# Four layers in one kernel: the high part of gate and query weights meets both parts of h in one product of 512 columns

## The reference

```python
h = _layernorm(x) * (1.0 + scale[:, None, :]) + shift[:, None, :]
p = h @ w_in[l]
u_f, z_f, cq, ckv, k_r, z_a = jnp.split(p, split_pts, axis=-1)
y_f = _fourier_mix(u_f, w_fmix[l]) * jax.nn.silu(z_f)
...
y_a = _mla_attention(q_nope, q_rope, k_nope, k_rope, v) * jax.nn.silu(z_a)
y = jnp.concatenate([y_f, y_a], axis=-1) @ w_out[l]

h = rms_norm(x, norm_g) @ w_in          # even: pooling, top-k attention
p_in, p_gate, dq, dk, dv, d_gate, iq, ik, iw = split_cols(h, EVEN_SPLITS)
h = rms_norm(x, norm_g) @ w_in          # odd: windowed attention with sinks
q, k, v, gate = split_cols(h, ODD_SPLITS)
```

## Time and profile before

| | |
|---|---|
| Median of three runs | 1638.18 us (1636.6 to 1639.8) |
| The profiled execution | 1637.07 us |
| Its span, first to last instruction | 1635.3 us |
| Busy: PE, PE weight loads, DVE, ACT | 1508.8, 1329.6, 1086.4, 706.7 us |
| Mean granted TensorE clock | 0.965 of 2.4 GHz |
| Read from HBM | 341.16 MB, 210 GB/s |
| Chain that ended last, by engine | PE 78%, DVE 8%, DMA 5%, ACT 4% |

### The profile page before, as it was taken

The page is one execution under the profiler, slowest core; times in us unless marked ns, Lnnn a source line. Parts: engine busy times, 40 slices in busy tenths (PEclk is TensorE's granted clock), DMA queues, the critical chain, the costliest instruction groups (busy, mean ns, idle before and its releaser), DMA issues.

```text
span 1635.3 us, 25215 instructions
## 1 busy us (share of the span) xinstructions
PE 1508.8 (92%) x9919; PEld 1329.6 (81%) x9919; DVE 1086.4 (66%) x1854; ACT 706.7 (43%) x1195; POOL 30.7 (2%) x56
## 2 busy tenths in 40 slices
PE   4888999989949999999968999999998999999998
PEld 0667788988839888998858998789987998879986
DVE  3426668889987757666676466884655667886553
ACT  1324234335326444444325344544544545655442
POOL 3000000000000000000000000010000000000000
PEclk8898999999979999999988999999999999999999
DMA  9996887998945766676546546427665553434662
GB/s 351 380 380 230 256 288 252 368 330 331 346 155 170 255 168 200 226 244 207 193 141 197 174 142 177 133 73 262 184 193 153 167 155 104 115 106 140 183 218 90
DMA packets 182437, 345.00 MB, mean 211 GB/s; under 512 B 28876, under 2 KB 43440, under 8 KB 181552
## 3 DMA queue, kind: packets, MB, share of 16 engines
q1 hardware_dynamic: 177744, 326.88, 61.7%
q0 software_dynamic: 4576, 16.52, 2.9%
HBM read 341.16 MB, written 2.20 MB: 210 GB/s over the span
## 4 chain that ended last, share of the span: by engine, by line
PE 78%; DVE 8%; DMA 5%; ACT 4%; issue 3%; SPq 2%; POOLq 0%; POOL 0%; DVEq 0%; ACTq 0%
PE PM L1359 65%; PE PB L1359 8%; DMA stg<-in_w_in 3%; SPq L1284 2%; ACT AR L1709 2%; DMA AR<-in_w_in 1%; ACT whi L1709 1%; DVE X L1934 1%; PE PB L1561 1%; PE PB L1533 1%; DVE AC L1934 1%; PE PB L1636 1%; DMA AR<-in_w_ada 1%; DVE wlo L2010 1%; DVE AR L1934 1%
## 5 line engine op out<-in xcount | busy, mean ns | idle before, releaser
L2010 DVE TENSOR_TENSOR wlo<-stg,whi 128x1024 fp32r<-128x1024 f32 (+2 forms) x421 | 500.1, 1197 | 350.3 <-ACT whi L1709 349.0
L1709 ACT ACTIVATE whi<-stg 128x1024 fp32r<-128x1024 f32 (+2 forms) x421 | 434.2, 1037 | 467.4 <-PE PM L1359 352.2
L1359 PE MATMUL PM<-Hh,whi 128*128 128x256 f32 x1824 | 528.0, 292 | 9.1 <-DVE wlo L2010 6.6
L1359 PE MATMUL PM<-Hh,wlo 128*128 128x256 f32 x1780 | 501.5, 285 | 0.0
L1359 PE MATMUL PM<-Hl,whi 128*128 128x256 f32 x1824 | 498.1, 285 | 0.0
L1359 PEld LDWEIGHTS PM<-Hh,whi 128*128 128x128 f32 x1824 | 353.2, 194 | 28.8 <-issue 12.4
L1359 PEld LDWEIGHTS PM<-Hh,wlo 128*128 128x128 f32 x1780 | 344.1, 193 | 0.0
L1359 PEld LDWEIGHTS PM<-Hl,whi 128*128 128x128 f32 x1824 | 343.1, 193 | 0.6
L1359 PE MATMUL PM<-whi,Hh 128*128 128x512 f32 (+1 forms) x576 | 224.3, 391 | 0.0
L1359 PE MATMUL PM<-wlo,Hh 128*128 128x512 f32 (+1 forms) x576 | 220.9, 385 | 0.0
L1359 PE MATMUL PM<-whi,Hl 128*128 128x512 f32 (+1 forms) x576 | 219.1, 385 | 0.0
(11 more groups left out here) (268 smaller groups left out, 1461.3 us busy)
## 6 DMA issues: line engine op xcount, KB each, us to landing
stg<-in_w_ada SPq DMA_DIRECT2D x162, 512.0 KB, 6.5
stg<-in_w_in SPq DMA_DIRECT2D x107, 512.0 KB, 5.4
stg<-in_even_w_in SPq DMA_DIRECT2D x80, 512.0 KB, 3.6
stg<-in_odd_w_in SPq DMA_DIRECT2D x72, 512.0 KB, 3.7
stg<-in_w_out SPq DMA_DIRECT2D x64, 512.0 KB, 5.0
stg<-in_even_w_out SPq DMA_DIRECT2D x32, 512.0 KB, 3.9
stg<-in_odd_w_out SPq DMA_DIRECT2D x32, 512.0 KB, 4.2
AR<-in_w_ada SPq DMA_DIRECT2D x30, 512.0 KB, 11.5
```

The lines of the kernel that those rows point to most:

```text
L1359: return e.matmul(out, l, r, start=start, stop=stop, skip_group_check=True)
L1709: return e.activation(out, x, f, **k)
L2010: e.tensor_tensor(wlo[s["slot"]][:, :, 0:n], stg[s["slot"]][:, :, 0:n], whi[s["hi"]][:, :, 0:n].bitcast(F32), ALU.subtract).then_inc(SEM[" ...
```

## The change

H becomes one tensor `H2` with the two parts of a k block side by side, so that 512 columns hold Hh and Hl of it. In a **wide** group the whi weights of a block stream over all 512 of them: one product gives whi by Hh in the left half of a bank and whi by Hl in the right half. wlo by Hh goes to the left half as before. A bank now holds one block instead of two, so a group has two blocks (256 columns), and a chunk is four k blocks of 256 columns: 4 x 2 x 2 = 16 products. The number of chunks stays the same. At the eviction the halves are added: ACT copies the right half to SBUF, DVE adds it. Gates of layers 1 to 3, queries and half of the indexer queries of layer 2, its indexer keys, and the queries of layer 3 become wide: 152 chunks, and the 8 chunks of the indexer keys with two k blocks each. Layer 0 stays narrow. Besides, `post` is now called for two blocks at a time, after four chunks.

```diff
+NARROW = (0,)
+WIDE2 = [unit("A", j, 0, j * 128) for j in range(2)]
...
+    def wide(self, w, c0, post, cols=None, units=WIDE2):
+        g = {}
+        nk = 4 if cols is None else 2
+        for q in range(KT // nk):
+            if cols is None:
+                src, n = [(0, 256, w, nk * q, c0)], 512
...
+                self.step("wide", q=q, nk=nk, pair=g["pair"], free=g["free"] if q == 0 else (), split=job["split"], hi=job["hi"],
+                          slot=job["slot"], units=units, h=[self.h[nk * q + i] for i in range(nk)])
...
     def gate_post(self, l, blocks):
         def post(pair, mm):
             if blocks[-1] == KT - 1:
-                self.y_split(range(2, 6), mm)
+                self.y_split(range(2, blocks[0] // 2), mm)
                 return lambda: gate(pair, mm)
...
-            for j in range(2):
+            for j in range(len(blocks) // 2):
                 b0 = blocks[2 * j]
                 self.drain(lambda: self.z[b0] is not None and self.z[b0 + 1] is not None)
...
+    def gates(self, l, w, c0, c1):
+        for b in range(0, KT, 4):
+            c = c0 + 128 * b if b < 8 else c1 + 128 * (b - 8)
+            if l in NARROW:
+                self.group([(w, c, 512)], A4, self.gate_post(l, list(range(b, b + 4))))
+            else:
+                for i in (0, 2):
+                    self.wide(w, c + 128 * i, self.gate_post(l, [b + i, b + i + 1]))
...
-        Hh = sb("Hh", [128, KT, S], F32R)
-        Hl = sb("Hl", [128, KT, S], F32R)
+        H2 = sb("H2", [128, KT, 2, S], F32R)
+        Hh, Hl = H2[:, :, 0, :], H2[:, :, 1, :]
...
+                        if s["nk"] == 4:
+                            dst = by_four(stg[slot])
+                            src = weights[w][k * 128:(k + 4) * 128, c0:c0 + n].rearrange("(k p) n -> p k n", p=128)
...
+                elif kind == "wide":
...
+                        for u in s["units"]:
+                            b, cols = PM[2 * s["pair"] + u["bk"]], slice(u["c0"], u["c0"] + u["n"])
+                            mm(b[0:u["n"], :], H[:, kk, cols], H2[:, k, :, :].rearrange("p j s -> p (j s)"), k == 0, False)
+                            ins = mm(b[0:u["n"], 0:S], L[:, kk, cols], Hh[:, k, :], False, k == KT - 1)
...
+                elif kind == "q_wide":
+                    q.wait_ge(s["mm"])
+                    q.wait_all(s["free"])
+                    for m in range(2):
+                        ins = act(ar(s["dst"] + m * S, S), (P0, P1)[m][:, S:2 * S])
+                    ins.then_inc(SEM["half"], 1)
                 elif kind == "gate":
                     q.wait_ge(s["mm"])
                     q.wait_all(s["tfree"])
+                    if s["fold"]:
+                        for m in range(2):
+                            ins = act(TMP[s["tmp"]][:, m * S:(m + 1) * S], (P0, P1)[m][:, S:2 * S])
+                        ins.then_inc(SEM["half"], 1)
+                        q.wait_ge(s["fold"])
...
                 elif kind == "gate":
                     pb, T, b0 = (P0, P1)[s["j"]], TMP[s["tmp"]], s["b0"]
+                    if s["fold"]:
+                        q.wait_ge(s["mm"])
+                        q.wait_ge(s["half"])
+                        e.tensor_tensor(P0[:, 0:S], P0[:, 0:S], T[:, 0:S], ALU.add)
+                        e.tensor_tensor(P0[:, S:2 * S], P1[:, 0:S], T[:, S:2 * S], ALU.add).then_inc(SEM["fold"], 1)
...
+                elif kind == "q_wide":
+                    q.wait_ge(s["half"])
+                    for m in range(2):
+                        x = ar(s["dst"] + m * S, S)
+                        ins = e.tensor_tensor(x, (P0, P1)[m][:, 0:S], x, ALU.add)
+                    ins.then_inc(SEM[s["sig"]], 1)
```

More of the change, by code:

```diff
@@ L59, in put, with unit @@
         self.free.append((b, signals))
+def unit(kind, bk, off, c0, n=128, t=0):
+    return dict(kind=kind, bk=bk, off=off, c0=c0, n=n, t=t)
+WIDE2 = [unit("A", j, 0, j * 128) for j in range(2)]
 class Plan:
@@ L163, in prep @@
         job["ld"] = ld
-        self.step("load", slot=slot, src=job["src"], free=free)
+        self.step("load", slot=slot, src=job["src"], nk=job.get("nk", 2), free=free)
         if job["mode"] == "split":
@@ L432, in y_split, with y_rest @@
         return c
-    def y_rest(self):
+    def y_rest(self, qs):
         self.drain()
@@ L684, in heads @@
                 self.z[8 + h + n] = a
[L686 to L689, removed]
+        self.gates(l, w, 1024, 2880)
         return begin
@@ L841, in value_iw @@
             self.banks.put(b, Tk["iw"])
-        self.group([(w, 5248, 64), (w, 3072, 128), (w, 5312, 16)],
-                   [unit("A", 0, 0, 0), unit("A", 1, 0, 128, 80)], ik_post)
+        self.wide(w, None, ik_post, [(w, 5248, 64), (w, 3072, 128), (w, 5312, 16)],
+                  [unit("A", 0, 0, 0), unit("A", 1, 0, 128, 80)])
         def scores():
@@ L878, in post @@
             def post(pair, mm):
-                for m in range(2):
-                    a = self.tick("q2_out")
-                    Tk["q", 4 * j + 2 * m] = Tk["q", 4 * j + 2 * m + 1] = a
-                self.step("iq_out", pair=pair, mm=mm, dst=Q2 + 4 * j * S, free=tuple(arf), sig="q2_out")
+                a = self.tick("q2_out")
+                Tk["q", 2 * j] = Tk["q", 2 * j + 1] = a
+                self.step("q_wide", half=self.tick("half"), pair=pair, mm=mm, dst=Q2 + 2 * j * S, free=tuple(arf), sig="q2_out")
                 return [a]
             return post
-        for j in range(2):
-            self.group([(w, 2048 + j * 512, 512)], A4, q_post(j))
+        for j in range(4):
+            self.wide(w, 2048 + j * 256, q_post(j))
         def p_post(j):
@@ L923, in even @@
             self.group([(w, j * 512, 512)], B2, p_post(j), pre=q_rinv if j == 0 else None)
-        for j in range(2):
-            self.group([(w, 1024 + j * 512, 512)], A4, self.gate_post(l, list(range(4 * j, 4 * j + 4))))
-        for j in range(2):
-            self.group([(w, 3200 + j * 512, 512)], A4, self.gate_post(l, list(range(8 + 4 * j, 12 + 4 * j))))
+        self.gates(l, w, 1024, 3200)
         return begin
@@ L969, in heads @@
                                               h // 2))
-        for j in range(4):
-            self.group([(w, j * 512, 512)], A4, q_post(j))
-        for j in range(4):
-            self.group([(w, 2560 + j * 512, 512)], A4, self.gate_post(l, list(range(4 * j, 4 * j + 4))))
+        for i in range(8):
+            self.wide(w, i * 256, q_post(i))
+        self.gates(l, w, 2560, 2560 + 1024)
         return begin
```

94 lines of the change are left out of this document (68 added, 26 removed).

## The result

The changed kernel takes **1643.84 us** (median of seven runs, 1642.18 to 1647.46), the kernel before 1637.27 us beside it (seven runs, 1635.85 to 1639.8). The ratio is 1.0037 with a 95% interval of 1.0026 to 1.0048: slower by 0.37%, or 6.6 us. The forecast was 1637.4 us and no change. The time lies within the range, on the slower side, which had 0.30.

A forecast was written before the change was run, and what follows sets the result against it. TensorE, busy for 92% of the span, was taken as the bound; -15.8 (products) + 9.0 (layer 2's piece) + 3.5 (clock) + 2.5 (layer 3's attention) = -0.8 us gave 1637.4 us, range 1630.5 to 1646.0.

The forecast's parts named there:

- the slower side: Whole kernel: the outcome of a time slower by over 0.2%, given a chance of 0.30.
- The products: TensorE's wide chunks: a pair takes 347 instead of 360 ns, 13 ns less for 1216 pairs, -15.8 us.
- The Trainium skill's 2.5 ns a product: TensorE's products: a warm product costs its columns and about 2.5 ns, so 3.0 us saved; the prediction went by 13 ns.
- The piece in layer 2: Layer 2's first gates: draining attention after four chunks leaves a piece without chunks; four then run at full price, +9.0 us.
- its clock: The piece in layer 2: TensorE idles 3.5 us, the clock falls to 1.2 GHz once or twice, +3.5 us.
- Loads and quiet evictions: Smaller DMA pieces, and gate evictions where no attention runs, hide behind TensorE's products: 0.
- Layer 3's attention: Layer 3's queries and gates beside attention: added evictions and waits cost +2.5 us; the stretch still shrinks 2 to 3 us.
- the layout alone: The wide form without the merge: layer 2's piece, its clock and layer 3's attention, 9.0 + 3.5 + 2.5 = 15.0 us.
- the merge saves almost nothing: Rival on the products: the fixed 13 ns are per 256 columns, not per product; 1650.2 us, chance 0.04.

The follow-up runs named there:

- k3_first: Changed kernel with only the first four gate blocks of layer 2 narrow again, in one group with one drain: 1634.07 us, ratio 0.9974 to the kernel before.
- k4_odd: Changed kernel with layer 3's queries and its gate blocks 0 to 7 narrow again: 1644.6 us, ratio 1.0036 to the kernel before.
- k2_three: Changed kernel with the wide layout kept but each 512-column product done as two of 256, undoing the merge: 1652.93 us, ratio 1.0092 to the kernel before.
- k10_hold: Changed kernel with layer 2's first wide gate group held, its eviction recorded with the second's after eight chunks: 1636.73 us, ratio 0.9984 to the kernel before.
- k7_cross: Changed kernel with one unit's wide product alternating with the other unit's narrow one, from each wide group's second chunk on: 1641.92 us (one run).

## Why the prediction was wrong

**The products: the step that failed.** It gave 1216 x 13 ns = 15.8 us for one fixed part less in each pair. In the changed kernel's stretches without attention a pair took 353.3 ns, not 347, and gave 6.7 ns: 1216 x 6.7 = 8.1 us. "I take the measured steps, since the mixed neighbours have their rows": those rows are single changes of width between two groups. A chunk is a long run in which wide and narrow alternate, and there was no row for that. Such a run has a rhythm of its own, at 347 or at 353 ns a pair. The forecast took the shorter one for all of them; in layer 1 of k3_first and k4_odd it was there, in the changed kernel's quiet stretches the longer one was. What chooses between them stays open. The text gave bounds from nothing to 16.4 us and chose close to the upper one.

The Trainium skill's 2.5 ns a product ("TensorE: Matmul & The Clock Gate", section "Wait — 56ns, not 53.3ns?") would have put the saving at 3.0 us, an estimate. The trace agrees with neither that nor with the forecast: k2_three shows 8.1 to 9.1 us.

**The piece in layer 2: right.** Forecast +9.0 and its clock +3.5, less 12 chunks x 0.1 us elsewhere in the stretch: +11.3. Measured +10.1, and in k4_odd, with the same orders there, +11.8. Its length (33.3 us) and the wait at its start (3.49 us) came as said. The clock's part came out smaller in this profile: one fall, with 3.2 us of products at half speed, costs at most 1.6 us, where 3.5 were taken. In k4_odd, with 8.8 us of products at the low level, it was up to 4.4. So 3.5 was inside what the clock does there. That the gate's eviction costs nothing here held for the changed kernel too, which has one in the piece (PE waits 2.57 us behind it; behind the two narrow gates before it waited 2.33), but it would not hold for two in a row (k10_hold).

**Loads and quiet evictions: right, 0.** PE was busy for 46.00 of 46 us, the gate's chain took 3.6 us, and in layer 1 k2_three needs 114.95 us where the kernel before needs 114.94.

**Layer 3's attention: right in size.** Forecast +2.5 for the layout; k2_three against before shows +3.2. The stretch did not shrink by 2 to 3 us as said, but grew by 2.5, because the shorter products gave less than the 5.0 us counted for its 48 chunks (384 pairs x 13 ns). At 0.053 us a chunk they are 2.5 us shorter, and from k2_three to the changed kernel the stretch lost only 0.7.

**Not forecast:** +1.0 us at layer 2's values, in the changed kernel and in k3_first, k10_hold and k4_odd alike. PE waits there for wlo twice, 0.25 and 0.45 us; the rest was not traced.

By the table of stretches the layout alone (k2_three less before) costs 12.5 us in layer 2's first gates, 3.2 in layer 3's attention and 0.8 at layer 2's values, 16.3 with the rest of the table; the merge gives 8.1. That is +8.2 us in the profiles and +6.6 by the medians, where the forecast had +15.0 and -15.8. The wrong step is worth 6.7 to 7.7 us, about all of the miss; that the layout's cost came so close, in spite of a clock that falls differently in each profile, is in part luck. Of the rivals, "the merge saves almost nothing" was the one on the right path: it was given 0.04, because a width-independent 13 ns seemed read off. About half of the saving was missing, as if that rival were half true, but not for its reason: 13 ns per 256 columns would make every pair 360 ns, and at the shorter rhythm it is 347.

## What to carry to other kernels

A step between two instructions holds for the neighbours that it was measured between: before using it for a new mix, look for a row with a run of that mix, not for single neighbours. Look at more than one place, too: one window of k7_cross said "bank", and another window of the same trace took it back. When products of unlike width would alternate, group them by width; here that costs two lines and held 348 ns a pair in every stretch without attention, though it moved the time by itself no further than the scatter. And when a change doubles the number of evictions, look first at those that stand in a drained part, where nothing covers a hand-over between engines, and leave that one group in its old form: here that edit alone turned a loss of 0.37% into a gain of 0.26%, and with the order of the products 0.39%.

## What the runs showed that was not expected

- A 512-column product and a 256-column product in turn took 346.7 or 353.3 ns as a pair, the longer one in a pattern of three pairs (1.06 us), and each held for tens of us without a break. Both were seen with the two products in one bank (changed kernel, k3_first) and in two (k7_cross). Narrow products alone kept their 0.120 us each. Why there are two rhythms, and what chooses, was not found.
- Groups of equal instructions in stretches with attention differed by up to 3 us between kernels with the same orders, and the stretches of low clock lay elsewhere in each: 97.6 against 95.9 us for layer 2's first gates. Differences of 1 or 2 us there need the runs, not one profile.
- Grouping the products by width moved the time by 1.4 us or less by itself, but by 2.6 us (1634.07 to 1631.48) once layer 2's piece was gone. From layer 1's gates on, these two profiles differ by 1.8 us (983.8 and 982.0). With intervals of about 2 us to each side, whether that is more than scatter stays open.
